# A state-space mixer in a two-block transformer kernel: the order of TensorE, VectorE and ScalarE at its two ends

## The reference

```python
def mamba2_mixer(h, w_in, conv_w, conv_b, dt_bias, a_log, d_skip, norm_g, w_out):
    proj = h @ w_in
    z = proj[..., :DI]                                    # DI = 2048
    xbc = proj[..., DI:DI + SSM_CONV_DIM]                 # then a conv of width 4 and silu
    ...
    y = ssd_chunked(xs * dt[..., None], dt * a, bm, cm)   # 8 groups of 256 columns, chunks of 128 tokens
    y = y + d_skip.astype(jnp.float32)[:, None] * xs
    y = y.reshape(bsz, seq, DI) * jax.nn.silu(z.astype(jnp.float32))
    yg = y.reshape(bsz, seq, G, DI // G)                  # G = 8
    yg = yg * lax.rsqrt(jnp.mean(yg * yg, axis=-1, keepdims=True) + EPS)
    y = yg.reshape(bsz, seq, DI) * norm_g.astype(jnp.float32)
    return y.astype(h.dtype) @ w_out                      # 2048 x 1024
```

## Time and profile before

| | us |
|---|---|
| median of 3 runs | 1574.6 (1573.8 to 1575.99) |
| the profiled execution | 1570.16 |
| its span | 1568.3 |
| TensorE busy in the span | 1542.8 (98%) |
| VectorE busy | 1101.7 (70%) |
| ScalarE busy | 828.7 (53%) |
| GpSimd busy | 55.7 (4%) |
| one slot of weights, issue to landing | 4.8 |

### The profile page before, as it was taken

How to read it: one execution, slowest core, us unless ns; L and a number is a source line. 1 busy time by engine, 2 the same in 40 slices (tenths; PEclk the granted TensorE clock), 3 DMA queues, 4 the chain that set the end, 5 groups by cost and what they waited for, 6 DMA issues and landing times.

```text
span 1568.3 us, 26675 instructions
## 1 busy us (share of the span) xinstructions
PE 1542.8 (98%) x10644; PEld 1346.7 (86%) x10644; DVE 1101.7 (70%) x1379; ACT 828.7 (53%) x1238; POOL 55.7 (4%) x69
## 2 busy tenths in 40 slices
PE   9999999999999999999999999999999998999999
PEld 8978899888888888888888888888889986788887
DVE  4865955776677767677776667776679938576765
ACT  7633755544446444457654446444466659554443
POOL 1000000000000000000000000000000036000000
PEclk9999999999999999999999999999999999999999
DMA  8332443555554555543355454555444550445553
GB/s 305 131 100 84 177 178 121 186 186 200 187 187 157 195 186 188 198 167 144 135 202 200 167 207 161 188 200 201 167 155 162 188 181 36 164 179 194 179 195 107
DMA packets 41028, 268.45 MB, mean 171 GB/s; under 512 B 5104, under 2 KB 7920, under 8 KB 9584
## 3 DMA queue, kind: packets, MB, share of 16 engines
q1 hardware_dynamic: 40240, 264.63, 47.5%
q0 software_dynamic: 704, 2.62, 0.4%
HBM read 265.66 MB, written 1.58 MB: 170 GB/s over the span
## 4 chain that ended last, share of the span: by engine, by line
PE 91%; DVE 4%; ACT 2%; DMA 2%; issue 1%; SPq 0%; POOL 0%; DVEq 0%; ACTq 0%
PE PS L627 25%; PE PS L559 15%; PE PS L560 15%; PE PS L561 15%; PE PS L630 13%; PE PS L840 1%; PE PS L856 1%; DMA raw_weights<-W 1%; PE PS L642 1%; PE PS L643 1%; PE PS L649 1%; PE PS L515 1%; DVE w_lo L1949 1%; ACT x_normed L1852 0%; PE PS L727 0%
## 5 line engine op out<-in xcount | busy, mean ns | idle before, releaser
L1949 DVE TENSOR_TENSOR w_lo<-raw_weights,w_hi 128x1024 fp32r<-128x1024 f32 x487 | 589.4, 1228 | 329.7 <-ACT w_hi L1357 328.4
L1357 ACT ACTIVATE w_hi<-raw_weights 128x1024 fp32r<-128x1024 f32 x488 | 506.5, 1055 | 276.8 <-PE PS L561 134.0
L627 PE MATMUL PS<-h_both,w_hi 128*128 128x512 f32 x1680 | 420.0, 392 | 0.0
L627 PEld LDWEIGHTS PS<-h_both,w_hi 128*128 128x128 f32 x1680 | 305.3, 189 | 56.1
L630 PEld LDWEIGHTS PS<-h_both,w_lo 128*128 128x128 f32 x1680 | 229.3, 191 | 16.3
L630 PE MATMUL PS<-h_both,w_lo 128*128 128x256 f32 x1680 | 234.4, 283 | 0.0
L559 PE MATMUL PS<-w_hi,g_hi 128*128 128x512 f32 x440 | 172.1, 391 | 0.0
L560 PE MATMUL PS<-w_lo,g_hi 128*128 128x512 f32 x440 | 172.1, 391 | 0.0
L561 PE MATMUL PS<-w_hi,g_lo 128*128 128x512 f32 x440 | 171.4, 390 | 0.0
L559 PE MATMUL PS<-h_both,w_hi 128*128 128x256 f32 x560 | 161.3, 288 | 1.9 <-DVE h_both L1975 1.4
L560 PE MATMUL PS<-h_both,w_hi 128*128 128x256 f32 x560 | 158.7, 283 | 0.0
(11 more groups left out here) (395 smaller groups left out, 1599.7 us busy)
## 6 DMA issues: line engine op xcount, KB each, us to landing
raw_weights<-W SPq DMA_DIRECT2D x243, 1024.0 KB, 4.8
raw_weights<-taps SPq DMA_DIRECT2D x2, 1024.0 KB, 7.2
h_both<-gated SPq DMA_DIRECT2D x8, 256.0 KB, 4.8
post_gain<-post_gains POOLq DMA_DIRECT2D x3, 512.0 KB, 3.7
x_resid<-x SPq DMA_DIRECT2D x2, 512.0 KB, 4.2
raw_weights<-W SPq DMA_DIRECT2D x2, 512.0 KB, 7.2
arena<-mem POOLq DMA_DIRECT2D x1, 1024.0 KB, 5.4
out<-x_resid SPq DMA_DIRECT2D x2, 512.0 KB, 2.7
```

The costliest lines, as they stand in the source:

```text
L627: mm(both_out, w_hi[:, slot, c * P:(c + 1) * P], h_both[:, :, c, :], start=c == 0, stop=False)
L1357: A(w_hi[:, n % H, :], raw[:, n % (2 * R), :], ACT.Copy).then_inc(S.hi_ready, 1)
L1949: v.tensor_tensor(w_lo[:, n % H, :], raw[:, n % (2 * R), :], w_hi[:, n % H, :].bitcast(F32), ALU.subtract).then_inc(S.lo_ready, 1)
```

## The change

On TensorE, front(0) and front(1) go from behind the sixth half of the second z product to behind the fifth. The first half of ssm_out becomes a function of its own (first_out_half): it waits for one chunk of h_lo instead of two, and bank by bank for the group loop's last additions. Each later half waits for its own chunk, and out_transposes 4 to 7 each stand one slot (two halves) later: four halves run ahead of out_transposes(4), and two between each further pair of sets.

On VectorE, group_scales loses its reciprocal to a function group_reciprocals; in the last but one pass of the loop own_in 12 and 13 go ahead of weighted_cb 14 and 15, the reciprocal goes ahead of carried_in(6), out_lo(0) between own_in 14 and 15; the second group_means goes ahead of out_lo(4) and the second reciprocal and scales behind it. On ScalarE three squares change places: 2G-6 goes from ahead of the first scales to behind out_hi(1), 2G-5 and 2G-4 behind out_hi(3). out_hi is not changed.

```diff
--- before.py
+++ after.py
@@ -1237,13 +1237,6 @@
             to_tokens(range(4))
             pe.wait_ge(S.z_ready2, 4)
             z_half = 2 * (FIRST["z"] + 4)
-            for j in range(6):
-                rows_half(z_half + j, h_hi[:, j, :], h_lo[:, j, :], 0, j == 0, False)
-                if j == 1:
-                    to_tokens(range(4, 8))
-                if j == 3:
-                    to_tokens(range(8, 10))
-
             def front(n):
 
                 g, t, b = n // 2, n % 2, n % 2
@@ -1293,10 +1286,17 @@
                     pe.wait_ge(S.g_lt, 2)
                 mm(PS[:, 7, 0:256], bcT[:, 8 + g, P:T], stT[:, g % 2, :], start=True, stop=True).then_inc(S.g_y, 1)
 
-            pe.wait_ge(S.sT_ready, 10)
-            pe.wait_ge(S.g_dx, 3)
-            front(0)
-            front(1)
+            for j in range(6):
+                rows_half(z_half + j, h_hi[:, j, :], h_lo[:, j, :], 0, j == 0, False)
+                if j == 1:
+                    to_tokens(range(4, 8))
+                if j == 3:
+                    to_tokens(range(8, 10))
+                if j == 4:
+                    pe.wait_ge(S.sT_ready, 10)
+                    pe.wait_ge(S.g_dx, 3)
+                    front(0)
+                    front(1)
             rows_last(z_half + 6, [h_hi[:, j, :] for j in (6, 7)], [h_lo[:, j, :] for j in (6, 7)], 0, S.z_part, S.z_part)
             for g in range(G):
                 if g == 0:
@@ -1322,19 +1322,35 @@
                                                    y_s[:, t, c * P:(c + 1) * P], ident)
                 last.then_inc(S.ysT_done, 1)
 
+            def first_out_half():
+
+                n = 2 * FIRST["ssm_out"]
+                pe.wait_ge(S.lo_ready, n + 1)
+                pe.wait_ge(S.ysT_ready, 1)
+                for t in range(TT):
+                    ts = slice(t * P, (t + 1) * P)
+                    for h in range(2):
+                        if t == 0:
+                            pe.wait_ge(S.g_sum, 3 * G - 2 + h)
+                        elif h == 1:
+                            pe.wait_ge(S.g_sum, 3 * G)
+                        hs = slice(h * 512, (h + 1) * 512)
+                        last = products(PS[:, 4 + 2 * t + h, :], (h_hi[:, 0, ts], h_lo[:, 0, ts]),
+                                        (w_hi[:, n % H, hs], w_lo[:, n % H, hs]), True, False)
+                last.then_inc(S.half_done, 1)
+
             for n in range(4):
                 out_transposes(n)
-            for n in range(8):
-                pe.wait_ge(S.ysT_ready, 2 * n + 2)
-                if n == 7:
-                    rows_last(2 * (FIRST["ssm_out"] + n), [h_hi[:, j, :] for j in (6, 7)],
-                              [h_lo[:, j, :] for j in (6, 7)], 4)
-                    break
-                for j in range(2):
+            first_out_half()
+            for n in range(7):
+                for j in range(1 if n == 0 else 0, 2):
                     c = (2 * n + j) % KC
-                    rows_half(2 * (FIRST["ssm_out"] + n) + j, h_hi[:, c, :], h_lo[:, c, :], 4, n == 0 and j == 0, False)
-                if n < 4:
-                    out_transposes(n + 4)
+                    pe.wait_ge(S.ysT_ready, 2 * n + j + 1)
+                    rows_half(2 * (FIRST["ssm_out"] + n) + j, h_hi[:, c, :], h_lo[:, c, :], 4, False, False)
+                if 1 <= n <= 4:
+                    out_transposes(n + 3)
+            pe.wait_ge(S.ysT_ready, 16)
+            rows_last(2 * (FIRST["ssm_out"] + 7), [h_hi[:, j, :] for j in (6, 7)], [h_lo[:, j, :] for j in (6, 7)], 4)
             unscaled(9)
             ffn(4)
 
@@ -1905,12 +1921,13 @@
                     gated_square(2 * g - 1)
             group_roots(0)
             state_in(G - 1)
-            gated_square(2 * G - 6)
             group_scales(0)
             for c in range(4):
                 out_hi(c)
-                if c % 2:
-                    gated_square(2 * G - 5 + c // 2)
+                if c == 1:
+                    gated_square(2 * G - 6)
+            gated_square(2 * G - 5)
+            gated_square(2 * G - 4)
             split(2 * FIRST["ssm_out"] + 2)
             gated_square(2 * G - 3)
             for c in range(4, KC):
@@ -2673,48 +2690,63 @@
                 ms_ = ysms[:, G * half:G * (half + 1)]
                 v.tensor_scalar(ms_, ms_, 1.0 / 256, 1e-6, ALU.mult, ALU.add).then_inc(S.ys_ms, 1)
 
-            def group_scales(half):
+            def group_reciprocals(half):
+
                 dve.wait_ge(S.ys_std, 5 * half + 1)
                 hs = slice(G * half, G * (half + 1))
                 v.reciprocal(ysr[:, hs], ysstd[:, hs]).then_inc(S.ys_ms, 1)
+
+            def group_scales(half):
+
                 dve.wait_ge(S.ys_ms, 2 * half + 2)
                 for g in range(4 * half, 4 * half + 4):
                     y = y_s[:, 0, g * 256:(g + 1) * 256]
                     v.tensor_scalar(y, y, ysr[:, 2 * g:2 * g + 1], None, ALU.mult).then_inc(S.ysn_ready, 1)
 
-            decayed(0)
-            weighted_cb(0)
-            weighted_cb(1)
-            split(2 * (FIRST["z"] + 8) + 1)
-            for g in range(G - 1):
-                decayed(g + 1)
-                if g < G - 2:
-                    weighted_cb(2 * g + 2)
-                    weighted_cb(2 * g + 3)
-                    own_in(2 * g)
-                else:
-                    group_means(0)
-                    weighted_cb(2 * g + 2)
-                    own_in(2 * g)
-                    weighted_cb(2 * g + 3)
-                own_in(2 * g + 1)
-                carried_in(g)
-            group_scales(0)
-            own_in(2 * G - 2)
-            own_in(2 * G - 1)
-            carried_in(G - 1)
-            for c in range(16):
-                if c in (2, 4):
-                    split(2 * FIRST["ssm_out"] + 1 + c // 2)
-                if c == KC:
-                    group_means(1)
-                    group_scales(1)
+            def out_lo(c):
+
                 if c >= KC:
                     split(2 * FIRST["ssm_out"] + c - KC + 4)
                 dve.wait_ge(S.ysT_hi, c // 2 * 2 + 2)
                 v.scalar_tensor_tensor(h_lo[:, c % KC, :], PS[:, c // 2 % 4, c % 2 * T:(c % 2 + 1) * T],
                                        pc("ssm_norm", c), h_hi[:, c % KC, :].bitcast(F32), ALU.mult, ALU.subtract)\
                     .then_inc(S.ysT_ready, 1)
+
+            decayed(0)
+            weighted_cb(0)
+            weighted_cb(1)
+            split(2 * (FIRST["z"] + 8) + 1)
+            for g in range(G - 2):
+                decayed(g + 1)
+                weighted_cb(2 * g + 2)
+                weighted_cb(2 * g + 3)
+                own_in(2 * g)
+                own_in(2 * g + 1)
+                carried_in(g)
+            decayed(G - 1)
+            group_means(0)
+            own_in(2 * G - 4)
+            own_in(2 * G - 3)
+            weighted_cb(2 * G - 2)
+            weighted_cb(2 * G - 1)
+            group_reciprocals(0)
+            carried_in(G - 2)
+            group_scales(0)
+            own_in(2 * G - 2)
+            out_lo(0)
+            own_in(2 * G - 1)
+            carried_in(G - 1)
+            out_lo(1)
+            split(2 * FIRST["ssm_out"] + 2)
+            for c in (2, 3):
+                out_lo(c)
+            split(2 * FIRST["ssm_out"] + 3)
+            group_means(1)
+            out_lo(4)
+            group_reciprocals(1)
+            group_scales(1)
+            for c in range(5, 16):
+                out_lo(c)
             residual(4, 1.0, "ssm_out", 7)
             unscaled(9, "ssm_out", 7)
             ffn(4)
```

## The result

The changed kernel takes 1587.07 us (median of 6, 1583.76 to 1588.82) against 1574.73 for the kernel before: a ratio of 1.0075, 95% interval 1.0064 to 1.0085, or +11.8 us (10.1 to 13.4) by that ratio. Slower, as forecast, but nearly twice the forecast +6.3, and above the range's end of 1583.6.

The account below looks back on a forecast made before the run. TensorE, busy 98% of the span, bounds the kernel, so only its waits count. The terms -0.9 - 1.0 - 2.3 + 10.5 = +6.3 us gave 1580.9 us from a median of 1574.6; range 1577.4 to 1583.6.

Parts of the forecast that it names:

- Part 1: Start of the group loop: fronts 0 and 1 one half of z sooner save 0.9 us.
- Part 2: Turn from the loop to ssm_out: half 0 starts 1.0 us sooner, range 0.7 to 1.5.
- The open price: VectorE's first group scale, 0.81 us beside GpSimd's gate(13): starting ahead of it might save up to 0.47 us more.
- Part 3: ssm_out: halves 2 and 3 fill TensorE's gap ahead of the second transposes, saving 2.3 us.
- Part 4: ssm_out halves 4, 6, 8, 10: weights split behind the later transposes, four TensorE stalls of 2.6 us, 10.5 us in all.
- covered: Odd halves of ssm_out: second w_lo of a pair ends 5.0 us behind the transposes' start, wanted at 5.7, no stall.
- rival D: Clock of TensorE falls after four gaps of 2.6 us, doubling one half each: 4 x 2.74, in all +17; 2%.

Follow-up runs that it names:

- experiment 7: Kernel before run once more, 1574.01 us; kernel before with only fronts 0 and 1 moved behind the fifth half of z, 1572.73 us (single executions).
- Experiments 1 and 2: Changed kernel, split ahead of the wait for the transposes: on ScalarE, even half only, 1573.42 us; both halves of a pair, ScalarE and VectorE, 1568.64 us.
- experiment 1: Changed kernel with ScalarE's w_hi split in out_hi put ahead of the wait for the transposes: 1573.42 us, ratio 0.9993 to the kernel before.
- experiment 3: Changed kernel with extra matmuls behind each of transposes 4 to 7: with 11, 1580.26 us, ratio 1.0040; with 4, 1579.60 us, ratio 1.0031.
- the remedy: Changed kernel with both halves of a pair split ahead of the wait for the transposes, on ScalarE and VectorE: 1568.64 us, ratio 0.9964.
- 11 fillers: Changed kernel with 11 extra matmuls of 512 columns behind each of transposes 4 to 7: 1580.26 us, ratio 1.0040.
- VectorE late with the reciprocal: Changed kernel, ScalarE's split ahead of the wait for the transposes, VectorE's behind it with one extra reciprocal before each of four splits: 1576.43 us, ratio 1.0015.
- transposes back a second time: Later execution of the changed kernel with the second transposes back behind halves 1, 3, 5 and 7: 1571.87 us.
- part 1 alone: Kernel before with only fronts 0 and 1 moved behind the fifth half of z: 1572.73 us, a single execution.

## Why the prediction was wrong

**Part 1** was right: 0.9 us forecast, 0.9 found in the profile and alone in experiment 7, for the reason given (the gate's last activation waits for the end of z).

**Part 2** was right within its bounds: 1.0 forecast, 0.7 to 1.5 as the range, 1.2 found (half 0 at z + 31.2, of 33.3 less 0.9). The open price went as the exclusive port lock of the Trainium skill ("SBUF — State Buffer", "Who interferes with whom") says, and only in part as I used it: the first scale now starts ahead of GpSimd's gate(13) (1329.50) and no longer takes the 0.81 us of the earlier trace rows: the next one starts 0.26 us behind it, and the gate takes 0.77 us where it took 0.73. The delay passed to the second scale,

```profile
1329.60 0.82 DVE L2704 TENSOR_SCALAR arena<-arena,small 128x256 f32<-128x256 f32 x1
```

so the four together take 1.61 us, as before. Of the up to 0.47 us that I had left open, the transposes of bank 0 got 0.3. They no longer wait for the scale: they stand behind two matmuls of TensorE's own, which waited for carried_in(6), a wait that I hadn't named. And own_in(14), behind all four scales, gained nothing.

```profile
1329.57 0.67 PE L1287 MATMUL PS<-arena 128*128 128x256 f32 x2 [0.27 <-DVE arena L2685]
1330.07 1.93 PE L1321 MATMUL PS<-ctab,arena 128*128 128x128 f32 x16
```

(The list of VectorE's work ahead of the first scale has seven instructions, not eight; nothing rests on it.)

**Part 3** was right: the wait of 2.3 us is gone.

**Part 4** was right in its mechanism and its size: four stalls, behind the sets of transposes, of 2.74 us against 2.6 forecast, 11.0 us in all against 10.5. Experiments 1 and 2 show that the place of the split, and nothing else, makes them. That the odd halves were "covered" was true of this kernel, though only by the stalls themselves, as experiment 1 showed.

**The step that failed is the clock**: the sum had it at nothing, and it stood only as rival D. I gave that 2%, on the single fact that the clock stayed at 1.00 behind the gap of 2.3 us in one profile. What the runs showed in its place: a fall behind each of the four stalls, 1.6 us each, 6.4 in all; fillers in the stalls took the falls away (experiment 3). There were two faults. I took one profile of an event of chance as a rule: experiment 7 shows that the same kernel falls behind the same gap in another execution, so the row could not exclude anything. And I carried it to longer gaps, 2.74 us, where it fell behind all four. With the four falls the sum would have been +6.3 + 4 x 1.6 = +12.7, against 12.8 in the profile and 11.8 by the ratio. The size of D was off as well: I priced a whole half at half speed (2.74 us), while eight matmuls ran slowly, 1.6 us.

The baseline had a part in it too. In the profile of before, the mixer has no fall; many other executions have more of them. Every execution comes with its mean granted clock, to 0.001, and one fall of 1.6 us is 0.001 of an execution. The 73 executions of the kernel before that the experiments were measured against have 0.998 on average, eight of them 1.000. The six of the changed kernel have 0.9948 on average and none more than 0.996, the price of four falls. As an estimate, the lost share times the time, that is 3.2 us of slow clock before and 8.2 after. The difference of 5.0 us and the stalls less the gains, 10.96 - 4.4 = 6.6, make +11.6, against 11.8 measured. For the remedy it is 0.9984 against 0.9979, 0.8 us, and 4.4 + 0.8 = 5.2 against 5.7. Where in those executions the clock fell is not recorded, so how much of the 3.2 us stands behind the gap of 2.3 us stays open.

## What stays open

In four profiles with the new start of the loop (the remedy, 11 fillers, VectorE late with the reciprocal, transposes back a second time) the clock also fell in the loop, from z + 6.0 to z + 9.4 in all four, where TensorE waits only in short pieces. In the remedy (us, busy, clock, DMA share, GB/s):

```profile
1301.80:1305.80 4.00, 3.39 (x28) 0.75 0.31 129
1305.80:1309.80 4.00, 4.00 (x62) 0.82 0.02 4
```

It costs 1.2 us: the first transposes stand at z + 30.35 there and at z + 29.1 without it. The other six profiles with the new start of the loop (part 1 alone among them) have none, and none of the four with the old start. Four of ten against none of four may be chance, or the new start may have made it likelier; no run here tells these apart. What decides between a fall and none, at a gap of 2.3 us or at the 3.0 us of 101.9 to 104.9, isn't visible in the trace either.

## What to carry to other kernels

When an instruction is moved on one engine, read what every other engine does behind its wait for it: the weights of the next halves were prefetched behind a wait for the transposes, on two engines, and moving the transposes later turned a prefetch into a stall that no changed line shows. Put a prefetch ahead of a wait that it doesn't need, and enough of it for the whole stretch that follows. And price a standstill of TensorE with the clock that may fall behind it, from more than one profile: here that added 1.6 us to each stall of 2.7.

## What was not expected of the hardware

- In ssm_out, behind a standstill of 2.7 to 3.5 us TensorE ran at 1.2 GHz six times in six, for 5 to 8 matmuls of 512 columns (0.43 us apart instead of 0.23); behind 2.2 to 2.3 us three times in five, among them both results from one and the same kernel; behind 1.9 us or less never in twenty. It is no rule for other places: one standstill of 3.0 us (changed kernel, 104.9) left the clock at 1.00, and waits of 1.11 and 0.77 us (kernel before, 480.7) had a slow stretch behind them.
- Four otherwise useless matmuls in each stall, 0.91 us of work, kept the clock at 2.4 GHz and saved 0.44% of the kernel's time (1.0031 against 1.0075).
- The slow stretch need not begin with the first matmul: in the second profile of before it began 0.9 us behind it (1341.32 to 1342.24).
